# A three-layer fp32 kernel on one core: five chunks of the modulation vectors by 512-column matmuls with silu(c) spread over the array, turned by VectorE, and twelve matmuls of constants at the start

## The chip, the cores and the metric

The kernel runs on one core of one Trainium2 chip. The metric is the device time of the whole program in microseconds. The program issues its instructions to TensorE (PE), VectorE (DVE), ScalarE (ACT), GpSimd (POOL) and SyncE (SP, which issues most transfers). All data are float32. Each fp32 matmul in the program shows in the trace as two matmul instructions, so counts of the trace are twice those of the program.

## What is computed

256 tokens of width 1024 go through three blocks. In each, a conditioning vector `c` gives shift, scale and gate vectors by a matrix, and these modulate the normed input:

```python
def first_block(x, c, w_mod, b_mod, ...):
    mod = silu(c) @ w_mod + b_mod                       # [1,1024] @ [1024,6144]
    shift1, scale1, gate1, shift2, scale2, gate2 = split(mod, 6)
    h = rms_norm(x, g_pre_mix) * (1 + scale1) + shift1
    y = hybrid_mixer(h, w_in, ...)                      # attention and gated linear attention
    x = x + gate1 * rms_norm(y, g_post_mix)
    h = rms_norm(x, g_pre_ffn) * (1 + scale2) + shift2
    y = moe_ffn(h, router_w, ...)                       # 32 experts, 4 per token
    return x + gate2 * rms_norm(y, g_post_ffn)
# the second block (mod = silu(c_2) @ w_ada_2 + b_ada_2, 3072 columns) and the third
# (two layers, silu(c_3) @ ada_w_3[l] + ada_b_3[l], 6144 columns each) have the same frame
# with other mixers and feed-forward parts
```

## The kernel before

The program is written by hand, engine by engine; each engine's instructions run in the order in which they are written, and semaphores join the engines (`e.wait_ge(*at(name))` waits for the instruction that was counted under that name). The stages come one after the other: `start`, `first` (the first block's mixer), `moe` (its experts), `second`, `even`, `ffn0`, `odd`, `ffn1`. The profile's lines for TensorE's dense matmuls are L792 (token-major, 512 columns) and L776 (feature-major, 256 columns); L735, L1152, L883 and L1208 are transposes; L1007, L1015 and L996 are the attention's.

**Modulation chunks.** The columns of all `mod` matrices that are needed are cut into chunks of 512, `ADA[0]`, `ADA[1]`, ... A chunk's weights are 1024 x 512, 2 MB, laid in a slot of the weight ring as 8 tiles of 128 rows (k = 0 to 7). A chunk is computed in one of two ways:

- By VectorE: `ada_acc_dve` multiplies the 8 tiles with silu(c) as a per-partition scalar and adds them (L608, L611, L616). TensorE then sums over the partitions with a vector of ones in `ada_sum_pe` (L625, four matmuls of one column each for a chunk of kind "cols").
- By TensorE alone, `ada_columns_pe` (L648): for each of the 4 groups of 128 columns and each of the 8 k, the 128 x 128 piece of weights is the stationary operand and one column of silu(c) is the moving one. So a chunk is 32 matmuls of one column, 64 in the trace. Chunks 1, 12, 13 and 15 are done so, and half of chunk 3 (columns 0 to 255; VectorE does the other half).

Both leave the chunk with its 128 features on the partitions, in four columns of a PSUM bank. `ada_put_dve` then adds the bias and puts it into `MOD` (L669, L672, L675).

**Chunk places.** Chunks 0 to 3 are the first block's first shift and scale; the `first` stage starts when they are there: `first_put_act` and `first_put_dve` (L475, L482) apply them to the turned input, and the small matmul L776 on `GR` (the gate's low rank projection) is the first that reads that. Chunk 12's two halves stand in the attention of token block 1 (`first_piece_pe`, s = 5 and s = 8), chunk 13's around a transpose after the linear attention (`first_pe`), and chunk 15's first half between the two norms' transposes (L883) at the end of `first`; its last two quarters stand after the router (L1979) and after the ranks (L1984 to L1988) in `moe_pe`, ahead of the first gather (L1521) of the experts.

**Weight ring and banks.** SP loads the weights into four slots in the order of use, each load waiting until the slot's last reader is done; for the experts two more slots are used, the tiles `GR` and `AUX`. The 4th load of expert weights takes the slot of chunk 15, and the loads into `GR` and `AUX` are queued behind it. PSUM's 8 banks are handed out in turn, and a bank waits for the readers of its last user.

**ACT's start.** ACT issues half of the small transfers of vectors, takes silu(c) from the turned `c` in the middle of them (L452), and issues the transfer `GR<-in_w_in` last (L457). POOL issues the other half. TensorE turns the vectors when all have landed (L498), behind chunk 1 and the sum of chunk 0.

Of the kernel before, what the change touches and what calls it, by code (L numbers as in the profile page):

```python
# [373 lines left out]
def programs(T, out, m, ps, sems, slots, at_c, at):  # L374
# [16 lines left out]
    GLRW = GR[:, 2, 0:128].rearrange("p (k n) -> p k n", k=8)  # L391
    VC = GR[0:24, 4, NV * 128:NV * 128 + 128]
# [49 lines left out]
    def start_act(e):  # L442
# [6 lines left out]
        for i, (dst, src, cleared) in enumerate(vector_pieces(0)):  # L449
            if i == N_PIECES[0] // 2:  # L450
                e.wait_ge(*at("c turned"))
                e.activation(CS[:, :], bank("c")[:, 0:24], ACT.Silu).then_inc(*act("cs"))  # L452
                act.leave("bank", "c")
            if cleared:
# [14 lines left out]
        act.name("first", "act")  # L469
        inputs_landed(e)  # L470

# [14 lines left out]
    def start_pe(e):  # L486
# [3 lines left out]
        e.wait_ge(*at("cs"))  # L490
        ada_columns_pe(e, 1, range(4))
        ada_sum_pe(e, 0)
        vectors_landed(e)
        e.wait_ge(*at("vr cleared"))
        for i in range(0, NV, 4):
# [3 lines left out]
            ins.then_inc(*pe("vectors turned", i))  # L499
        e.wait_ge(*at("first", "xn"))  # L500
        turn_pe(e, "first", lambda t, k: m.first.XN[:, t, cols(k)], 8)
        ada_sum_pe(e, 2)
        ada_columns_pe(e, 3, (0, 1))
        e.wait_ge(*at("ada acc", 3))
        for f in range(2, 4):
            ins = e.matmul(bank("ada", 3)[:, f:f + 1], AC2[:, 0, cols(f)], ones[:, 0:1], start=True, stop=True,
                           skip_group_check=True)
        ins.then_inc(*pe("ada summed", 3))
        bank.drop("ada", 3)
# [75 lines left out]
    BY_COLUMNS = (1, 12, 13, 15)  # L585
    SIDE, BEFORE, last_of = {}, {}, {}
    for n in range(len(ADA)):
        if n not in BY_COLUMNS:
# [50 lines left out]
    def ada_columns_pe(e, n, fs):  # L639

        w = ring.tile(1024, 512, "ada", n)
        if fs[0] == 0:
            bank.take(e, "ada", n, hold=True)
            e.wait_ge(*at("w", "ada", n))
        b = bank("ada", n)
        for f in fs:
            for k in range(8):
                ins = e.matmul(b[:, f:f + 1], w[:, k, cols(f)], CS[:, ADA[n][3] + k:ADA[n][3] + k + 1], start=k == 0, stop=k == 7,  # L648
                               skip_group_check=True)
        if n == 3:  # L650
            ins.then_inc(*pe())
            pe.leave("w", "ada", n)
        elif fs[-1] == 3:
            ins.then_inc(*pe("ada summed", n))
            pe.leave("w", "ada", n)
            bank.drop("ada", n)

    def ada_put_dve(e, n):
        kind, _, _, _, j, rest, _ = ADA[n]
        b = bank("ada", n)  # L660
        e.wait_ge(*at("ada summed", n))
        if kind == "cols":
# [5 lines left out]
            if j < 2:  # L668
                e.tensor_tensor(o, b[:, 0:4], bv, ADD).then_inc(*dve())  # L669
                dve.leave("bank", "ada", n)  # L670
            else:
                e.scalar_tensor_tensor(out=o, in0=b[:, 0:4], scalar=1.0, in1=bv, op0=ADD, op1=ADD).then_inc(*dve())  # L672
                dve.leave("bank", "ada", n)
                own(e, dve)
# [413 lines left out]
    wi1 = T["w_in"][0]  # L1088
    R1, U1 = F1.XN[:, :, 0:512], F1.XN[:, :, 512:768]
# [2135 lines left out]
```

## Time and profile before

| | |
|---|---|
| median of 3 runs | 2635.36 us (2631.52 to 2641.18) |
| profiled execution, its own time | 2640.11 us |
| its span in the trace | 2638.3 us |
| TensorE busy | 2353.4 us, 89% of the span |
| VectorE busy | 844.8 us, 32% |
| ScalarE busy | 412.4 us, 16% |
| mean granted TensorE clock | 0.931 of full |
| moved by DMA | 655.50 MB, mean 248 GB/s |

The chain of work that ended last is TensorE's for the greater part. Between about 330 us and 1330 us the 16 DMA engines are busy 91% to all of the time with the experts' weights; ahead of that and behind it TensorE is busy nearly without a gap. The granted clock is one of two levels: 1.00 is 2.4 GHz, 0.50 is 1.2 GHz.

### The profile page before, as it was taken

Reading aid. Unit: us, or ns where it says so; the run is one execution under the profiler, and the core shown is the slowest. Engines: PE = TensorE matmul, PEld = TensorE weight load, DVE = VectorE, ACT = ScalarE, POOL = GpSimd, SP = SyncE. Lnnn points to the kernel's source line nnn. Section 1 sums busy time; section 2 is a strip of 40 time slices with the busy share of each in tenths; the row PEclk is TensorE's granted clock in tenths of the full one; section 3 lists DMA queues with packets and bytes.
Section 4 is the critical chain, followed back from the end, with each engine's and each line's share of the span. In section 5 each row is a group of like instructions: output and inputs, shape, how many; then the busy total and the mean of one; then the engine's idle time right before and its main releaser. Section 6 shows DMA issues by size and latency. Waiting matters only on the chain. (4 is left out here: it accounts for less than half of the span.)

```text
span 2638.3 us, 25405 instructions
## 1 busy us (share of the span) xinstructions
PE 2353.4 (89%) x9952; PEld 1375.0 (52%) x9952; DVE 844.8 (32%) x1734; ACT 412.4 (16%) x889; POOL 115.9 (4%) x81
## 2 busy tenths in 40 slices
PE   6998989888899888888879989898779998989998
PEld 5565633333333333333337678655648763646873
DVE  4554312211122111122236443643366301332301
ACT  1212201111111111111122311112221001221100
POOL 1000000001000010000000000000300000000000
PEclk9977799999999999999989998889889999989999
DMA  8753468999989999999976720464236543323441
GB/s 314 263 217 138 177 245 322 381 412 406 411 305 378 409 397 412 403 409 412 401 300 248 255 80 17 179 247 179 96 128 235 180 152 126 132 86 120 160 143 65
DMA packets 212255, 655.50 MB, mean 248 GB/s; under 512 B 8518, under 2 KB 13182, under 8 KB 195540
## 3 DMA queue, kind: packets, MB, share of 16 engines
q1 hardware_dynamic: 208368, 647.86, 64.8%
q0 software_dynamic: 1712, 3.60, 0.4%
q8 instruction: 119, 1.95, 0.3%
q10 hardware_dynamic: 2004, 1.67, 0.2%
q14 instruction: 52, 0.43, 0.0%
HBM read 652.05 MB, written 1.05 MB: 248 GB/s over the span
## 5 line engine op out<-in xcount | busy, mean ns | idle before, releaser
L1558 PE MATMUL ps<-w,XE 128*64 128x512 f32 x1536 | 363.0, 628 | 66.5 <-DMA w<-in_w_gate_up 63.0
L776 PE MATMUL ps<-HF,w 128*128 128x256 f32 x1408 | 312.7, 385 | 1.8 <-DVE CF L2854 1.8
L776 PEld LDWEIGHTS ps<-HF,w 128*128 128x128 f32 x1408 | 271.8, 194 | 43.6 <-issue 5.7
L1558 PEld LDWEIGHTS ps<-w,XE 128*64 128x64 f32 x1536 | 122.8, 144 | 292.5 <-issue 288.5
L1588 DVE TENSOR_TENSOR T<-ps,BB 128x512 f32<-128x512 f32 x64 | 44.3, 692 | 616.9 <-PE ps L1558 616.9
L611 DVE SCALAR_TENSOR_TENSOR AUX<-w,CS,AUX 128x512 f32<-128x512 f32 (+1 forms) x228 | 169.8, 745 | 8.1
L792 PE MATMUL ps<-w,AF 128*128 128x512 f32 x352 | 151.6, 593 | 1.8 <-DVE AF L2876 1.8
L792 PE MATMUL ps<-w,HT 128*128 128x512 f32 (+1 forms) x352 | 152.8, 589 | 0.3 <-DVE S L1403 0.3
L776 PE MATMUL ps<-HT,w 128*128 128x256 f32 x640 | 146.8, 388 | 5.5 <-DVE dqk L2291 3.7
L1629 PE MATMUL ps<-GR,AT 128*64 128x512 f32 x256 | 120.9, 628 | 31.4 <-DMA AUX<-in_w_down 31.1
L1629 PE MATMUL ps<-w,AT 128*64 128x512 f32 x512 | 121.8, 619 | 18.3 <-DMA w<-in_w_down 17.9
L776 PEld LDWEIGHTS ps<-HT,w 128*128 128x128 f32 x640 | 123.0, 195 | 25.8 <-issue 9.0
L1629 PE MATMUL ps<-AUX,AT 128*64 128x512 f32 x256 | 121.4, 630 | 0.0
L1493 POOL PARTITION_BROADCAST BB<-BR x32 | 73.6, 2299 | 967.3 <-DMA BR<-in_b_gate_up 948.7
L1558 PE MATMUL ps<-GR,XE 128*64 128x512 f32 x256 | 113.3, 595 | 0.4 <-DVE ACCM L1666 0.4
L1558 PE MATMUL ps<-AUX,XE 128*64 128x512 f32 x256 | 113.3, 595 | 0.0
L792 PEld LDWEIGHTS ps<-w,AF 128*128 128x128 f32 x352 | 66.7, 190 | 85.9 <-issue 83.2
L792 PEld LDWEIGHTS ps<-w,HT 128*128 128x128 f32 x352 | 67.0, 202 | 75.8 <-issue 75.1
L1598 ACT ACTIVATE T<-T 128x256 f32<-128x256 f32 x70 | 30.8, 441 | 441.6 <-DVE T L1571 441.6
L1629 PEld LDWEIGHTS ps<-GR,AT 128*64 128x64 f32 x256 | 35.6, 144 | 108.6 <-issue 108.6
L792 PE MATMUL ps<-w,HO 128*128 128x512 f32 x192 | 85.6, 604 | 1.0 <-ACT st L846 1.0
L1629 PEld LDWEIGHTS ps<-w,AT 128*64 128x64 f32 x512 | 39.7, 141 | 88.3 <-issue 78.6
(568 smaller groups left out, 2666.9 us busy)
## 6 DMA issues: line engine op xcount, KB each, us to landing
w<-in_w_gate_up SPq DMA_DIRECT2D x96, 2048.0 KB, 15.7
w<-in_w_down SPq DMA_DIRECT2D x32, 2048.0 KB, 19.3
w<-in_ada_w SPq DMA_DIRECT2D x24, 2048.0 KB, 7.9
w<-in_ffn_w_in SPq DMA_DIRECT2D x20, 2048.0 KB, 7.9
w<-in_w_in SPq DMA_DIRECT2D x17, 2048.0 KB, 9.3
GR<-in_w_gate_up SPq DMA_DIRECT2D x16, 2048.0 KB, 18.1
AUX<-in_w_gate_up SPq DMA_DIRECT2D x16, 2048.0 KB, 22.8
GR<-in_w_down SPq DMA_DIRECT2D x16, 2048.0 KB, 10.0
```

What stands on the lines that cost most here:

```text
L611: e.scalar_tensor_tensor(out=acc, in0=w[:, k, lo:], scalar=c, in1=acc, op0=MUL, op1=ADD).then_inc(*dve())
L776: ins = e.matmul(out_, w[:, k, c:c + n], HT[:, k, :], start=k == 0, stop=k == kc - 1, skip_group_check=True)
L792: ins = e.matmul(out_, HT[:, k0 + k, cols(t)], w[:, k, c:c + n], start=start and k == 0, stop=stop and k == kc - 1, skip_group_check=True)
L1493: e.partition_broadcast(FM.BB[0:n, :], FM.BR[32 * j:32 * j + 1, :], n).then_inc(*pool(x, "bias"))
L1558: ins = e.matmul(b[j * n:j * n + n, :], FM.XE[:, side(x), 4 * kh + k, j * n:j * n + n], ring.tile(512, 1024, "gu", ex_, h, kh, x[0])[:, k, ...
L1588: e.tensor_tensor(FM.T1[:, :], bank(x, "gu", q), FM.BB[:, q * 512:q * 512 + 512], ADD).then_inc(*dve())
L1598: e.activation(FM.T2[:, :], v[:, :, 0], ACT.Sigmoid, scale=1.702).then_inc(*(wide["act"] if len(key) > 1 else act)(x, "sig", *key))
L1629: ins = e.matmul(b[j * n:j * n + n, :], FM.AT[:, 4 * d + k, j * n:j * n + n], ring.tile(512, 1024, "down", ex_, d, x[0])[:, k, 512 * hf:51 ...
```

## The change

Chunks 1, 12, 13, 15 and the half of chunk 3 are computed with the operands exchanged. ScalarE spreads silu(c) into a tile `CSB` (part of `GR`): for each k a block of 128 x 128 in which all 128 columns are the same column of silu(c). That block is stationary and the weights' tile of 128 x 512 (256 for chunk 3) is moving. A chunk is then 8 matmuls of 512 columns, which leave its 512 values in each partition of a whole bank. VectorE takes them out of it by four fused multiplies with the identity, summed along the row (`ada_turn_dve`), into four columns of `st`, ahead of the former `ada_put_dve`.

With it come:

- ScalarE writes `CSB` for silu(c) between the small transfers, and for silu(c_2) after chunk 3 (`spread_act`); it copies it into `CSB2` (the tile `att_p`, which is not used any more by then) in `first_act` after the first head norm, for chunk 15.
- 12 matmuls of constants with 256 columns stand on TensorE behind the transpose of `c`. Nothing reads their result.
- On TensorE the turned vectors go ahead of chunk 1.
- The sum of chunk 3's second half gets a bank of its own ("3b"), copied to `st` by VectorE.
- Chunk 12's two parts are k = 0 to 3 and k = 4 to 7, chunk 13's too; chunk 15's three parts are k = 0 to 2, 3 to 5 and 6 to 7, at the same places.

```diff
@@ start_act
                 e.activation(CS[:, :], bank("c")[:, 0:24], ACT.Silu).then_inc(*act("cs"))
                 act.leave("bank", "c")
+                own(e, act)
+                spread_act(e, 0, CSB)
...
         act.name("first", "act")
+        e.wait_ge(*at("ada summed", 3))
+        spread_act(e, 8, CSB)
         inputs_landed(e)
+    def spread_act(e, ccol, dst):
+        e.activation(dst, CS[:, ccol:ccol + 8].unsqueeze(2).broadcast_to([128, 8, 128]), ACT.Copy).then_inc(
+            *act("spread", ccol))
@@ start_pe
         e.transpose(b[:, 0:24], VC, ident[0:24, 0:24]).then_inc(*pe("c turned"))
-        e.wait_ge(*at("cs"))
-        ada_columns_pe(e, 1, range(4))
-        ada_sum_pe(e, 0)
+        b = bank.take(e, "warm")
+        for _ in range(12):
+            ins = e.matmul(b[:, 0:256], ident, CT[:, 0:256], start=True, stop=True, skip_group_check=True)
+        ins.then_inc(*pe())
+        pe.leave("bank", "warm")
         vectors_landed(e)
...
             ins.then_inc(*pe("vectors turned", i))
+        e.wait_ge(*at("spread", 0))
+        ada_rows_pe(e, 1, CSB)
+        ada_sum_pe(e, 0)
         e.wait_ge(*at("first", "xn"))
         turn_pe(e, "first", lambda t, k: m.first.XN[:, t, cols(k)], 8)
         ada_sum_pe(e, 2)
-        ada_columns_pe(e, 3, (0, 1))
+        ada_rows_pe(e, 3, CSB, n_cols=256)
+        b = bank.take(e, "ada", "3b")
         e.wait_ge(*at("ada acc", 3))
@@
-    def ada_columns_pe(e, n, fs):
+    def ada_rows_pe(e, n, spread, ks=range(8), n_cols=512):
         w = ring.tile(1024, 512, "ada", n)
-        if fs[0] == 0:
+        if ks[0] == 0:
             bank.take(e, "ada", n, hold=True)
             e.wait_ge(*at("w", "ada", n))
...
+        for k in ks:
+            ins = e.matmul(bank("ada", n)[:, 0:n_cols], spread[:, k, :], w[:, k, 0:n_cols], start=k == 0, stop=k == 7,
+                           skip_group_check=True)
+        if ks[-1] == 7:
+            ins.then_inc(*pe("ada rows", n))
+            if n_cols == 512:
+                pe.name("ada summed", n)
             pe.leave("w", "ada", n)
             bank.drop("ada", n)
+
+    def ada_turn_dve(e, n, fs):
+        e.wait_ge(*at("ada rows", n))
+        for f in fs:
+            e.tensor_tensor_reduce(TURN if n < 15 else m.moe.T2[:, 0:128], bank("ada", n)[:, cols(f)], ident, 1.0, 0.0, MUL, ADD, st[:, 50 + f:51 + f]).then_inc(
+                *dve())
+            own(e, dve)
+        dve.leave("bank", "ada", n)
 
     def ada_put_dve(e, n):
         b = bank("ada", n)
+        if n in BY_ROWS:
+            ada_turn_dve(e, n, range(2 if n == 3 else 4))
+            b = st[:, 50:54]
         e.wait_ge(*at("ada summed", n))
+        if n == 3:
+            e.tensor_copy(st[:, 52:54], bank("ada", "3b")[:, 2:4]).then_inc(*dve())
+            dve.leave("bank", "ada", "3b")
+            own(e, dve)
@@ first_piece_pe
-            ada_columns_pe(e, 12, (0, 1))
+            e.wait_ge(*at("spread", 8))
+            ada_rows_pe(e, 12, CSB, range(4))
...
-            ada_columns_pe(e, 12, (2, 3))
+            ada_rows_pe(e, 12, CSB, range(4, 8))
@@ first_pe
-        ada_columns_pe(e, 13, (0, 1))
+        ada_rows_pe(e, 13, CSB, range(4))
         e.wait_ge(*at("hn1", 0, "out"))
         turn_half_pe(e, "gla turned", 0, 512)
-        ada_columns_pe(e, 13, (2, 3))
+        ada_rows_pe(e, 13, CSB, range(4, 8))
...
         norm_turn_pe(e, m.moe, "moe", 0)
-        ada_columns_pe(e, 15, (0, 1))
+        e.wait_ge(*at("spread", "again"))
+        ada_rows_pe(e, 15, CSB2, range(3))
         norm_turn_pe(e, m.moe, "moe", 1)
@@ first_act
             headnorm_act(e, ("hn1", t), F1.XN[:, t, 0:512], 4, F1.XN[:, 0, 512:1024], st[:, 44 + 4 * t:48 + 4 * t])
+            if t == 0:
+                e.activation(CSB2, CSB, ACT.Copy).then_inc(*act("spread", "again"))
@@ moe_pe
-        ada_columns_pe(e, 15, (2,))
+        ada_rows_pe(e, 15, CSB2, (3, 4, 5))
         b = bank.take(e, "ranks")
...
-        ada_columns_pe(e, 15, (3,))
+        ada_rows_pe(e, 15, CSB2, (6, 7))
```

On TensorE the program before begins with these rows (the program's own counts, half of the trace's; `w_2` is chunk 1's slot, `w_4` chunk 3's):

```order
L489 MATMUL ps<-CT,GR 128x24
L648 MATMUL ps<-CS,w_2 128x1 x32
L625 MATMUL ps<-CT,AUX 128x1 x4
L498 MATMUL ps<-CT,GR 128x128 x5
L735 MATMUL ps<-CT,XN 128x128 x16
L625 MATMUL ps<-CT,AUX 128x1 x4
L648 MATMUL ps<-CS,w_4 128x1 x16
L506 MATMUL ps<-CT,AUX 128x1 x2
L776 MATMUL ps<-HT,GR 16x256 x8
```

The changed program begins on TensorE so:

```order
L499 MATMUL ps<-CT,GR 128x24
L502 MATMUL ps<-CT 128x256 x12
L510 MATMUL ps<-CT,GR 128x128 x5
L660 MATMUL ps<-w_2,GR 128x512 x8
L639 MATMUL ps<-CT,AUX 128x1 x4
L763 MATMUL ps<-CT,XN 128x128 x16
L639 MATMUL ps<-CT,AUX 128x1 x4
L660 MATMUL ps<-w_4,GR 128x256 x8
L522 MATMUL ps<-CT,AUX 128x1 x2
L804 MATMUL ps<-HT,GR 16x256 x8
```

The vectors' transposes moved ahead of chunk 1, and the matmuls of one column became matmuls of 512 and 256. From the router on, TensorE's rows before are these (L1979 is the router, L1984 to L1988 the ranks, L1521 the gather):

```order
L1979 MATMUL ps<-RW,HT_41 128x32 x16
L648 MATMUL ps<-CS,w_1 128x1 x8
L1984 MATMUL ps<-sl,CT 128x32
L1985 MATMUL ps<-sl,CT 128x32
L1986 MATMUL ps<-sl,CT 128x32
L1987 MATMUL ps<-sl,CT 128x32
L1988 MATMUL ps<-sl,CT 128x32
L648 MATMUL ps<-CS,w_1 128x1 x8
L1521 MATMUL ps<-PG,XN_40 128x128 x16
```

In the changed program the same place reads:

```order
L2012 MATMUL ps<-RW,HT_41 128x32 x16
L660 MATMUL ps<-w_1,att_p 128x512 x3
L2017 MATMUL ps<-sl,CT 128x32
L2018 MATMUL ps<-sl,CT 128x32
L2019 MATMUL ps<-sl,CT 128x32
L2020 MATMUL ps<-sl,CT 128x32
L2021 MATMUL ps<-sl,CT 128x32
L660 MATMUL ps<-w_1,att_p 128x512 x2
L1554 MATMUL ps<-PG,XN_40 128x128 x16
```

Nothing moved there; the parts of chunk 15 stand where they stood, in three and two matmuls. On VectorE the start of the changed program has these rows where the one before had two `TENSOR_TENSOR MOD<-ps,VT` in a row (L673 is the multiply with the identity and the read of its sum; L696 puts chunks 0 and 1, L698 and L703 chunk 2):

```order
L696 TENSOR_TENSOR MOD<-ps,VT 128x4
L673 ISA GR,st<-ps,CT 128x128
L673 ISA st 128x1
L673 ISA GR,st<-ps,CT 128x128
L673 ISA st 128x1
L673 ISA GR,st<-ps,CT 128x128
L673 ISA st 128x1
L673 ISA GR,st<-ps,CT 128x128
L673 ISA st 128x1
L696 TENSOR_TENSOR MOD<-st,VT 128x4
L698 SCALAR_TENSOR_TENSOR MOD<-ps,VT 128x4
L703 TENSOR_TENSOR MOD<-MOD,VT 128x4
```

The four multiplies are queued between the put of chunk 0 and that of chunk 2.

## Rows read from the trace of the kernel before

**Rows 1.** The page: TensorE's granted clock in 40 equal slices.

```profile
PEclk9977799999999999999989998889889999989999
```

**Rows 2.** Timeline of TensorE, 8 to 70 us: start us, us, engine line operation.

```profile
20.40 13.79 PE L648 MATMUL ps<-CS,w 128*128 128x1 f32 x64 [11.70 <-DMA w<-in_w_mod]
...
39.96 0.95 PE L625 MATMUL ps<-CT,AUX 128*128 128x1 f32 x8
...
49.52 5.45 PE L776 MATMUL ps<-HT,GR 128*16 128x256 f32 x16 [2.01 <-ACT HT L475]
54.90 14.00 PE L792 MATMUL ps<-w,HT 128*128 128x512 f32 x32
```

**Rows 3.** Timeline of VectorE, 20 to 50 us.

```profile
31.56 0.69 DVE L616 TENSOR_TENSOR AUX<-AUX 128x512 f32<-128x512 f32 x1
...
40.94 0.16 DVE L672 SCALAR_TENSOR_TENSOR MOD<-ps,VT 128x4 f32<-128x4 f32 x1 [2.96 <-PE ps L625]
```

**Rows 4.** Windows: stretch, us, busy (instructions) of PE, PEld, DVE, ACT, POOL, clock, DMA, GB/s.

```profile
43.00:53.00 10.00, 7.18 (x27) 4.80 (x27) 4.55 (x11) 1.02 (x2) 0.00 (x0) 0.50 1.05 387
55.00:69.00 14.00, 14.00 (x33) 6.07 (x34) 8.83 (x17) 0.00 (x0) 0.00 (x0) 1.00 0.13 50
...
183.00:189.00 6.00, 6.00 (x39) 4.53 (x37) 4.46 (x7) 0.00 (x0) 0.00 (x0) 1.00 0.24 49
190.00:203.00 13.00, 11.94 (x43) 8.45 (x45) 3.17 (x6) 1.19 (x2) 0.00 (x0) 0.50 0.71 268
...
224.00:233.00 9.00, 9.00 (x34) 7.45 (x34) 4.61 (x8) 1.32 (x3) 0.00 (x0) 0.50 0.19 41
...
252.00:284.00 32.00, 25.73 (x120) 25.36 (x121) 11.77 (x47) 5.74 (x16) 6.22 (x5) 0.50 0.26 75
298.00:314.00 16.00, 15.70 (x74) 5.41 (x73) 5.33 (x12) 4.92 (x12) 0.00 (x0) 1.00 0.01 5
```

**Rows 5.** DMA by queue (queue, kind: packets, MB, share), 22 to 24 us.

```profile
q10 hardware_dynamic: 1, 0.00, 0.0%
```

**Rows 6.** Timeline of TensorE, 155 to 204 us.

```profile
170.09 4.54 PE L648 MATMUL ps<-CS,w 128*128 128x1 f32 x32 [0.58 <-DVE att_m L1045]
...
175.38 5.68 PE L792 MATMUL ps<-w,HT 128*128 128x512 f32 x8
...
186.89 4.17 PE L648 MATMUL ps<-CS,w 128*128 128x1 f32 x32
190.92 1.95 PE L1015 MATMUL ps<-va,att_p 128*128 128x64 f32 x8
```

**Rows 7.** Timeline of TensorE, 216 to 290 us.

```profile
219.66 3.63 PE L648 MATMUL ps<-CS,w 128*128 128x1 f32 x32
...
223.62 6.54 PE L648 MATMUL ps<-CS,w 128*128 128x1 f32 x32
230.02 5.74 PE L792 MATMUL ps<-w,HT 128*128 128x512 f32 x8
...
255.25 1.95 PE L883 MATMUL ps<-CT,XN 128*128 128x128 f32 x8
263.47 7.01 PE L1979 MATMUL ps<-RW,HT 128*128 128x32 f32 x32 [6.27 <-issue]
270.29 3.55 PE L648 MATMUL ps<-CS,w 128*128 128x1 f32 x16
...
279.25 6.73 PE L1521 MATMUL ps<-PG,XN 128*128 128x128 f32 x32
```

**Rows 8.** Timeline of VectorE, 216 to 281 us.

```profile
227.05 0.69 DVE L1083 TENSOR_TENSOR O<-O,rg 128x512 f32<-128x512 f32 x1
...
253.66 1.29 DVE L876 TENSOR_SCALAR XN<-X,st 128x512 f32<-128x512 f32 x2
...
272.65 0.19 DVE L2054 CUSTOM_DVE_ANT_0 G<-w,sl 128x32 f32<-128x32 f32 x1
...
276.06 0.19 DVE L2063 SCALAR_TENSOR_TENSOR rk<-ps,sl 128x32 f32<-128x32 f32 x1 [1.93 <-PE ps L1988]
```

## The prediction on record

> **What bounds the kernel now.** I first read the page's clock line [rows 1]: nearly everywhere TensorE is granted nine tenths or all of full speed, but slices 3 to 5 (132 to 330 us) show 7. The changed chunks stand there and at the start, so I read TensorE's timeline from 0 to 290 us [rows 2, 6, 7]. From 20 us to 255 us TensorE is the engine that sets the end: its own gaps are a few of 1 to 2 us, the largest being the wait for the first weights up to 20.40 and 2.01 us for ScalarE at 49.52 [rows 2]. Then I cut the same time into windows for the clock [rows 4]. It is at 1.00 in the dense stretch 55 to 69 us and at 183 to 189, and at 0.50 (1.2 GHz) at 43 to 53, 190 to 203, 224 to 233 and 252 to 284 us. Each of these begins about 2 to 4 us after one-column matmuls L648 began: at 40.8 us behind the row of L625 at 39.96, at 186.89, at 219.66 and between the two transposes of L883 [rows 2, 6, 7]. TensorE was busy for all 6 us of 183 to 189, and the level fell all the same. Behind that, at half rate, stand dense matmuls that cost more than they would: the 8 of L792 at 230.02 took 5.74 us, where 32 at full rate took 14.00 us, 3.5 us for 8 [rows 2, 7].
>
> What the experts add is a question of where the stream of their weights starts. At 298 to 314 us the DMA engines stand still, share 0.01, while TensorE works 15.70 of 16 us [rows 4]: the slots are full, and their release by TensorE sets when the stream goes on. So what TensorE gains before 298 us moves the whole stream and reaches the end.
>
> **The price of a chunk itself** hardly changes. A half chunk by columns is 32 instructions: 3.63 us at full rate (113 ns each) [rows 7]; at half rate 13.79 / 64 = 215 ns each, 6.9 us [rows 2]. A half chunk by rows is 8 instructions of 512 columns, at full rate 14.00 / 32 = 437 ns each [rows 2], 3.5 us; at 1.2 GHz twice that, 7.0 us. The profile's clock reads 1.00 from 20 to 34 us, before its first record, but a one-column matmul that takes 215 ns there and 113 ns later says that this is 1.2 GHz. So what counts is at which level a chunk runs and what level it leaves behind. Dense work of this form (L792, full rows, 512 columns) holds 1.00 for as long as it runs [rows 4]; I take it that rows of chunks do the same.
>
> **Start.** Before: chunk 1 from 20.40 to 34.1, the sum of chunk 0, the vectors and the input turned, the sum of chunk 2 at 39.96 to 40.9; VectorE puts chunk 2 at 40.94 [rows 2, 3]; 49.52 is 8.6 us later. After: the constants' 24 instructions of 256 columns cost 24 x 0.22 = 5.3 us at full and 10.5 us at half rate, from about 8.7 us, so they end between 14 and 19.2 us, ahead of 20.4, when chunk 1's weights are there (that wait is a DMA's and stays). The vectors: ScalarE's queue q10 has one packet left after 22 us [rows 5], and its last issue, 1024 small pieces of `w_in`, is behind the vectors; so they land before 22 us, most likely by 17, the 1.1 us by which the spread delays them included. Bound: if at 23, 3.5 us are lost. I take 17, and the five transposes are done before 20.4. Chunk 1 by rows is then 16 x 0.437 = 7.0 us at full rate; the gap of some 2 us after the constants may let the level fall, and then about 4 us pass at half rate, 9 us in all. So it ends at 27.4 to 29.4. The sum of chunk 0 (0.95 us) and 16 transposes at full rate (about 2.1) end at 30.5 to 32.5, and the sum of chunk 2 can't start before VectorE has it at 31.56 + 0.69 = 32.25 [rows 3]. It ends at 33.3, instead of 40.9: 7.6 us, 7.2 with the unlucky phase. From there the chain is as before but for VectorE's additions in it: two multiplies with the identity of chunk 3 in place of TensorE's wait and one copy. The nearest row is the fused multiply of 128x32 at 0.19 us, next instruction after 0.23 [rows 8], the upper bound a 128x512 operation at 0.69 us [rows 3]; I take 0.35 us each for 128x128 and lose 0.5 us in all (0.2 to 1.2). The four of chunk 1, 1.4 us, lie in the 2 us in which VectorE waits for the sum of chunk 2. **Start: -6.9 us** (-3.4 to -7.5).
>
> **Chunk 12.** First half at 170.09: 4.54 us become 3.5, and L792 behind it 5.68 becomes 3.5, since the level doesn't fall; with the small attention pieces between, 10.8 us become 7.6: -3.2. Second half at 186.89: 4.17 becomes 3.5, -0.6. Behind it, from 190.92 to about 199.5, stand the attention's last pieces and a row sum at half rate [rows 4, 6] that would take 4.7 us at full. But they are thin themselves, so the level may fall again within them: -2.7 of the possible -4. TensorE's short wait for VectorE's `O` behind them stays. VectorE's four multiplies (1.4 us, at most 2.8) stand before its copy of `att_p`, and TensorE has 3.7 us of other work before it needs that. **-6.5 us** (-3.2, if only the first half's effect comes, to -9).
>
> **Chunk 13.** First half 3.63 against 3.5. Second half 6.54 becomes 3.5, and L792 behind it 5.74 becomes 3.5 [rows 7]. VectorE's head norm, which these wait for, is done at 227.05 + 0.69 = 227.7 [rows 8]; the transpose that needs it comes at 223.6 + 7.0 = 230.6. ScalarE's copy into `CSB2` (1 us) lies in a wait. **-5.0 us** (0 to -5.3).
>
> **Chunk 15.** Its first part lies in the wait for VectorE's L876 (253.66 to 254.95) and saves only that TensorE comes 0.3 us late at 255.25 and transposes in 1.95 us for about 1.05: **-1.0 us** (0 to -1.2). The second part is on the path, since VectorE waits 1.93 us for the ranks behind it [rows 8]. The router before it is thin and leaves the level at half, as now [rows 4, 7]. Six instructions of rows at half rate for about 4 us and then full: 4.6 us, instead of 3.4: +1.2. If the level then is full, the ranks take 1.2 for 2.1 us, the last part 1.75 for 3.4, and the gather (6.73 us) about 4.2. From the ranks' end VectorE needs 1.9 us for what the gather waits for, so it begins 0.2 us after the last part; all in all TensorE ends the gather 3.5 us earlier. If the level rises only within the gather, it is -0.5, and if never, +2. **-2.5 us** (+2 to -3.5).
>
> **Sum.** 6.9 + 6.5 + 5.0 + 1.0 + 2.5 = 21.9 us. Against the profiled execution: 2640.1 - 21.9 = 2618.2 us. That execution is 4.75 us above the median of the runs, so in terms of the median 2635.4 - 21.9 = 2613.5, and I say 2614.
>
> **A rule against it.** TensorE was busy in 6.00 of the 6 us ahead of 189 us, and the level was 0.50 directly after [rows 4]. The Trainium skill, "TensorE: Matmul & The Clock Gate", Part 1, says that the gate follows how busy TensorE has been, and that sustained activity releases the throttle. By that rule taken plainly a one-column stream is as good as a dense one, and the change buys nothing but its rearrangement. The trace here disagrees, if "busy" means the engine's busy time, but it leaves open why the level falls.
>
> **Rivals.**
>
> (a) *The levels stay where they are*: something other than the chunks lets the level fall (the thin attention pieces, the norms). Then at the start chunk 1 costs 14.0 us at half rate and only the five transposes of the vectors move out of the path (1.2 us by the 8 in 1.95 us [rows 7]), less 0.5 on VectorE; chunk 12 is 0; chunk 13 +0.5 (7.0 for 6.54); chunk 15 +1.9 and +0.1. Total +1.8 us: 2637. The thin L1015 and L1007 behind 186.89 speak for it, the 1.00 under L792 from 55 to 69 us, and the fall behind each of the four streams of L648 alike, against it. The rule above would give this one. Chance 7%.
>
> (b) *Part of it*: the start and chunk 13 come (11.9 us), but in chunk 12's and 15's surroundings thin work drops the level anyway: 2635.4 - 12 = 2623, or 2619 to 2627. For it: L1007, L1015, L996, the router are all thin. Chance 22%.
>
> (c) *Slower*: full-array matmuls that start from half rate don't raise it soon. If all halves of 12, 13 and 15 run at 7.0 us and so does each L792 of 8 behind them, chunk 12 costs 14.0 for 8.7 plus 1.3 + 3.4 us behind it, chunk 13 14.0 for 10.2 plus 1.3, chunk 15 +2; with a start of -1 that is +15 us: 2650. It decides from the point at which less than a third of the rows run at full rate. Against it: L792 holds 1.00 over 14 us [rows 4], and the level rose under L776 and L792 after 49.52. Chance 4%.
>
> (d) *Hidden*: the experts' stream starts by something that isn't moved, so that what comes after 280 us keeps its time. Then nothing remains, 2635. The idle DMA at 298 to 314 us speaks against it. Chance 4%.
>
> **Numbers.** The forecast holds 63%, (a) to (d) the 37% left. A difference under 0.5%, 13.2 us, is about what a measurement of this kernel can't tell from none. Its own range is 2606 (26 us, all best ends) to 2621; (b) reaches to 2627, and a range to there leaves (a), (c) and (d) out, 15%; at its low end it goes to 2605. Faster by over 0.5% (under 2622) is all of the forecast and six tenths of (b): 0.76; same is the rest of (b), (a), (d), and a quarter of (c): 0.21; slower 0.03.
>
> **What would show it.** Features of `first` (L804 now) start at 42 to 43 us; the first chunk's matmuls L660 at 20.4 us last 7 to 9 us; clock 1.00 from there through 190 less 7 us, and no stretch of 0.50 between the two halves of chunk 13 and the expert norm; the gather ends by about 264 instead of 286 us; the DMA's idle stretch before the experts' stream shifts by the same 22 us, and from then on the two traces run in parallel. I am wrong if the constants or the vectors end after 20.4 us, if VectorE's multiplies take over 0.7 us each, or if the level falls during the rows.

## The result: 1.0% faster, ratio 0.9899

The changed kernel takes 2607.05 us, the median of 4 runs (2603.8 to 2615.2), against 2633.44 us for the one before in the same comparison. The ratio is 0.9899, with a 95% interval of 0.9868 to 0.9931. The forecast was 2614 us (2605 to 2627), 21.4 us under the median of before; measured are 26.4. A second set of 6 runs of the changed kernel on another occasion gave 2612.32 us against 2635.32, 23.0 us less, a ratio of 0.9907 (0.9881 to 0.9933).

The profiled execution took 2603.8 us with a span of 2602.0, 36.3 us less than the span before. Only 22.6 us of that come from the stretch that the change touches; where the rest comes from is told behind the experiments.

### The profile page after: what moved, and what is told of

Same layout as the page of the kernel before. It is cut to its first block and busy times, and to the rows that moved or that the text cites. A ratio compares the mean times of both kernels' runs of the same rounds, so it can differ in the third digit from the quotient of the medians.

```text
span 2602.0 us, 25084 instructions
## 1 busy us (share of the span) xinstructions
PE 2324.2 (89%) x9768; PEld 1330.8 (51%) x9768; DVE 850.8 (33%) x1771; ACT 415.1 (16%) x892; POOL 115.8 (4%) x81
## 5 line engine op out<-in xcount | busy, mean ns | idle before, releaser
L1591 PE MATMUL ps<-w,XE 128*64 128x512 f32 x1536 | 362.5, 627 | 66.4 <-DMA w<-in_w_gate_up 63.0
L1591 PEld LDWEIGHTS ps<-w,XE 128*64 128x64 f32 x1536 | 124.3, 144 | 290.3 <-issue 286.4
L820 PE MATMUL ps<-w,AF 128*128 128x512 f32 x352 | 151.6, 593 | 1.8 <-DVE AF L2909 1.8
L820 PE MATMUL ps<-w,HT 128*128 128x512 f32 (+1 forms) x352 | 147.1, 572 | 0.3 <-DVE S L1436 0.3
L804 PEld LDWEIGHTS ps<-HT,w 128*128 128x128 f32 x640 | 124.1, 197 | 26.3 <-issue 9.1
L1591 PE MATMUL ps<-GR,XE 128*64 128x512 f32 x256 | 113.3, 595 | 0.4 <-DVE ACCM L1699 0.4
L1591 PE MATMUL ps<-AUX,XE 128*64 128x512 f32 x256 | 113.3, 595 | 0.0
L820 PEld LDWEIGHTS ps<-w,AF 128*128 128x128 f32 x352 | 66.7, 190 | 85.9 <-issue 83.2
L820 PEld LDWEIGHTS ps<-w,HT 128*128 128x128 f32 x352 | 64.7, 195 | 72.8 <-issue 72.0
L1662 PEld LDWEIGHTS ps<-GR,AT 128*64 128x64 f32 x256 | 36.3, 147 | 106.8 <-issue 106.8
L820 PE MATMUL ps<-w,HO 128*128 128x512 f32 x192 | 85.6, 604 | 1.0 <-ACT st L874 1.0
## 6 DMA issues: line engine op xcount, KB each, us to landing
AUX<-in_w_gate_up SPq DMA_DIRECT2D x16, 2048.0 KB, 22.2
```

Of the source, the lines that this page charges most:

```text
L804: ins = e.matmul(out_, w[:, k, c:c + n], HT[:, k, :], start=k == 0, stop=k == kc - 1, skip_group_check=True)
L820: ins = e.matmul(out_, HT[:, k0 + k, cols(t)], w[:, k, c:c + n], start=start and k == 0, stop=stop and k == kc - 1, skip_group_check=True)
L1591: ins = e.matmul(b[j * n:j * n + n, :], FM.XE[:, side(x), 4 * kh + k, j * n:j * n + n], ring.tile(512, 1024, "gu", ex_, h, kh, x[0])[:, k, ...
L1662: ins = e.matmul(b[j * n:j * n + n, :], FM.AT[:, 4 * d + k, j * n:j * n + n], ring.tile(512, 1024, "down", ex_, d, x[0])[:, k, 512 * hf:51 ...
```

## The profile after

The mean granted clock is 0.943 in place of 0.931. The page's clock line, in 40 equal slices, against [rows 1]:

```profile
PEclk9998999999999999999989989999789999989999
```

Slices 3 to 5 went from 7 to 9 or 8; a 7 further back, in slice 29, is new.

TensorE's timeline from 0 to 50 us, as in [rows 2] (start us, us, engine line operation, idle before and what ended it):

```profile
8.65 7.85 PE L502 MATMUL ps<-CT 128*128 128x256 f32 x24
17.07 0.77 PE L510 MATMUL ps<-CT,GR 128*128 128x128 f32 x5 [0.57 <-DMA GR<-in_ffn_conv_b]
20.57 8.70 PE L660 MATMUL ps<-w,GR 128*128 128x512 f32 x16 [2.73 <-DMA w<-in_w_mod]
...
32.55 1.02 PE L639 MATMUL ps<-CT,AUX 128*128 128x1 f32 x8 [0.69 <-DVE MOD L696]
...
42.20 6.31 PE L804 MATMUL ps<-HT,GR 128*16 128x256 f32 x16 [2.18 <-ACT HT L485]
```

The features start at 42.20 instead of 49.52, 7.3 us earlier. The vectors' last transfer ends TensorE's wait at 17.07, and they are turned before chunk 1's weights are there at 20.57. VectorE's part, by its timeline from 32 to 41 us:

```profile
32.40 0.28 DVE L673 CUSTOM_DVE_ANT_0 GR<-ps,CT 128x128 f32<-128x128 f32 x1
...
32.72 0.29 DVE L673 CUSTOM_DVE_ANT_0 GR<-ps,CT 128x128 f32<-128x128 f32 x1
```

One multiply with the identity starts 0.32 us behind the other; four take 1.3 us.

The windows of the changed kernel (columns as in [rows 4]):

```profile
20.00:22.00 2.00, 1.43 (x2) 0.84 (x3) 0.99 (x2) 0.00 (x0) 0.00 (x0) 0.59 1.10 362
24.00:40.00 16.00, 13.01 (x65) 9.12 (x63) 13.02 (x36) 1.02 (x2) 0.00 (x0) 1.00 1.04 387
42.00:46.00 4.00, 3.80 (x10) 1.34 (x11) 0.00 (x0) 0.68 (x1) 0.00 (x0) 0.50 1.07 390
...
160.00:162.00 2.00, 0.00 (x0) 0.00 (x0) 0.00 (x0) 2.00 (x9) 0.00 (x0) 0.58 1.04 385
168.00:186.00 18.00, 17.89 (x72) 9.82 (x71) 10.15 (x23) 0.00 (x0) 0.00 (x0) 1.00 0.38 131
188.00:190.00 2.00, 1.96 (x10) 1.66 (x10) 1.29 (x2) 0.60 (x1) 0.00 (x0) 0.50 1.03 418
192.00:236.00 44.00, 40.96 (x164) 20.45 (x160) 26.86 (x68) 14.48 (x37) 0.00 (x0) 1.00 0.46 168
240.00:255.00 15.00, 10.55 (x37) 8.51 (x38) 4.65 (x28) 1.93 (x3) 1.58 (x3) 0.50 0.10 20
256.00:264.00 8.00, 7.24 (x49) 5.51 (x47) 6.13 (x20) 2.09 (x6) 4.54 (x2) 1.00 0.44 111
```

From 160 to 162 us TensorE stands still, and the level falls. From 168 to 186 us, with the second half of chunk 12 in it, the level is 1.00, and only behind that it falls for some 3 us. The stretch of 44 us at 1.00 from 192 to 236 us holds all of chunk 13; before, the same work had 0.50 for 9 us [rows 4]. The router and the second part of chunk 15 run at 0.50 as before. Now the timeline from 150 to 265 us, against [rows 6, 7]:

```profile
163.67 5.40 PE L660 MATMUL ps<-w,GR 128*128 128x512 f32 x8 [7.10 <-DMA w<-in_w_ada]
...
178.78 3.60 PE L660 MATMUL ps<-w,GR 128*128 128x512 f32 x8
...
207.31 3.60 PE L660 MATMUL ps<-w,GR 128*128 128x512 f32 x8
...
211.18 3.60 PE L660 MATMUL ps<-w,GR 128*128 128x512 f32 x8
214.62 3.60 PE L820 MATMUL ps<-w,HT 128*128 128x512 f32 x8
...
236.93 1.24 PE L911 MATMUL ps<-CT,XN 128*128 128x128 f32 x8 [1.89 <-DVE XN L904]
244.45 7.01 PE L2012 MATMUL ps<-RW,HT 128*128 128x32 f32 x32 [6.28 <-issue]
251.27 5.11 PE L660 MATMUL ps<-w,att_p 128*128 128x512 f32 x6
...
259.57 3.81 PE L1554 MATMUL ps<-PG,XN 128*128 128x128 f32 x32 [0.35 <-DVE mxc L2103]
```

The first line is new: TensorE is ready for chunk 12 at 156.6 us and waits 7.10 us for its weights. SyncE's timeline shows when they are issued:

```profile
148.66 0.37 SPq L194 DMA_DIRECT2D w<-in_w_out  x1
149.07 29.43 SPq L194 DMA_DIRECT2D w<-in_w_ada  x3
```

They stand directly behind 2 MB of `w_out`, and both have to come in; the row in [rows 6] had 0.58 us of wait at the same place. The half chunk behind the wait begins at half rate and takes 5.40 us.

## The experiments

Two numbers are read from each run besides the time: when the first gather starts (279.25 us before [rows 7]), and when SyncE issues the last load of an expert's weights into `GR` (1329.48 us before, 1303.61 in the changed kernel). The second is behind all that the change touches and before the stages that follow.

**The change without its constants.**

```diff
-        b = bank.take(e, "warm")
-        for _ in range(12):
-            ins = e.matmul(b[:, 0:256], ident, CT[:, 0:256], ...)
```

> The change without its 12 matmuls of constants. Theory 1 (the constants buy nothing): in the changed kernel the clock is back at half rate within 2 us after they and the vectors' transposes end, and stands at 0.59 and 0.55 in the first 4 us of chunk 1, as it would without them. Then chunk 1 starts at about 20.6 us and takes 8.7 to 9.6 us, and the features' first matmul (L776 before, L804 after) starts within 1 us of 42.2 us; time equal to the change, 2604 to 2610. Theory 2 (they keep the clock up for chunk 1): chunk 1 takes 12 us or more, the features start at 45 us or later, and the time is 3 us or more above the change.

Measured: 2613.48 us, ratio 0.9915 (0.9894 to 0.9936). Its timeline of TensorE:

```profile
17.17 1.33 PE L505 MATMUL ps<-CT,GR 128*128 128x128 f32 x5 [8.50 <-DMA GR<-in_ffn_conv_b]
20.49 9.62 PE L655 MATMUL ps<-w,GR 128*128 128x512 f32 x16 [1.99 <-DMA w<-in_w_mod]
...
42.55 5.32 PE L799 MATMUL ps<-HT,GR 128*16 128x256 f32 x16 [2.18 <-ACT HT L485]
```

Chunk 1 takes 9.62 us in place of 8.70, and the features start at 42.55 in place of 42.20. Even this isn't the constants' doing: with them chunk 1 took between 8.70 and 10.17 us in the profiles of the eight kernels here that have the same start. The last load is issued at 1302.89 us, no later than in the changed kernel, and the ratio lies within the intervals of the change. Theory 1 holds: the constants buy nothing that can be seen. The time itself, 2613.48 us, is above the 2604 to 2610 that was expected, but the kernel before was slower on that occasion too (2638.65 against 2633.44 us), so the ratio is what compares.

**The start alone**, chunks 12, 13 and 15 by columns:

```diff
-            ada_rows_pe(e, 12, CSB, range(4))
+            ada_columns_pe(e, 12, (0, 1))
```

and so for the other halves.

> Only the start of the change: chunks 1 and 3 by rows, constants and vectors ahead; chunks 12, 13 and 15 by columns as before. Theory 1 (the gains of the two places add): the features start at 42.2 us as in the change and the time is about 7 us under before, 2626 to 2629. Theory 2 (the earlier start is taken back later by a wait for weights, as the changed kernel waits 7.1 us for chunk 12's): TensorE comes to chunk 12 at most 6 us earlier than before and the time is within 3 us of before.

**The later part alone**, the start as before:

```diff
-        ada_rows_pe(e, 1, CSB)
+        ada_columns_pe(e, 1, range(4))
```

with the order of before, and chunk 3 by columns.

> Only the later part of the change: the start as before, chunks 12, 13 and 15 by rows. Theory 1 (the level of the clock): the first gather ends about 15 us earlier than before, the gap between this and the whole change is the start's 7 us, and the time is 2612 to 2616. Theory 2 (the later gain needs the earlier start's phase of the clock): less than 8 us under before, 2625 or more.

Measured: the start alone 2625.07 us, 0.9945 (0.9925 to 0.9965); the later part alone 2620.5 us, 0.9923 (0.9903 to 0.9943). The two ratios together make 0.9868, the whole change measured 0.9899 and 0.9907, so they add within their intervals. The traces say more about where. From the start alone, TensorE:

```profile
42.55 5.36 PE L821 MATMUL ps<-HT,GR 128*16 128x256 f32 x16 [2.18 <-ACT HT L483]
...
164.30 5.79 PE L676 MATMUL ps<-CS,w 128*128 128x1 f32 x32 [1.86 <-DMA w<-in_w_ada]
...
274.20 5.74 PE L1567 MATMUL ps<-PG,XN 128*128 128x128 f32 x32
```

Of 7.0 us at the features 5.8 are left at chunk 12 and 5.1 at the gather. From the later part alone:

```profile
51.71 5.33 PE L812 MATMUL ps<-HT,GR 128*16 128x256 f32 x16 [1.92 <-ACT HT L483]
...
172.20 3.67 PE L653 MATMUL ps<-w,GR 128*128 128x512 f32 x8 [0.63 <-DMA w<-in_w_ada]
...
266.34 2.05 PE L1562 MATMUL ps<-PG,XN 128*128 128x128 f32 x16
```

Here the features start 2.2 us later than before though the program is the same up to there (the level of the clock fell at another place), and the gather starts 12.9 us earlier: 15.1 us come between the two. By these rows both theories 1 hold: each part gives its own gain, and the later one doesn't need the earlier.

The times fit less well. The start alone was expected 7 us under before; 0.9945 is 14.5 us (9 to 20), while its profile has 5.1 us at the gather. That profile is of the slowest of the six runs, 11 us above their median. The later part alone was expected at 2612 to 2616 and took 2620.5, in ratio 20 us (15 to 26), with the gather's end 14.0 us earlier in the trace. What fills these gaps isn't shown; how much the stretches behind the change vary by themselves is told further below.

**Wide columns.** The operands are turned back, the weights' pieces stationary, 32 matmuls a chunk as before; what moves is a block of 128 equal columns of silu(c). VectorE copies four columns.

```diff
-        for k in ks:
-            ins = e.matmul(bank("ada", n)[:, 0:n_cols], spread[:, k, :], w[:, k, 0:n_cols], ...)
+        for f in fs:
+            for k in range(8):
+                ins = e.matmul(bank("ada", n)[:, cols(f)], w[:, k, cols(f)], spread[:, k, :], ...)
```

> The change with the operands turned back: the weights' 128x128 pieces are stationary again, 32 matmuls a chunk as before, but each moves the 128 equal columns of the spread silu(c) in place of one column. VectorE copies four columns out of the bank in place of four multiplies. Theory 1 (what counts is that the stream is dense, so that the clock stays at full rate behind it): a half chunk of 12 or 13 takes 3.5 to 3.8 us, the clock is 1.00 between the two halves of chunk 13 and behind them, and the time is that of the change within 4 us, 2603 to 2611. Theory 2 (what counts is fewer matmuls and weight loads): the time goes back towards that of the start alone, 2620 or more.

Measured: 2613.38 us, ratio 0.9899 (0.988 to 0.9919). A window of the clock, and TensorE's timeline:

```profile
192.00:236.00 44.00, 41.20 (x225) 26.61 (x223) 25.53 (x57) 14.51 (x37) 0.00 (x0) 1.00 0.47 170
```

```profile
20.48 9.01 PE L661 MATMUL ps<-GR,w 128*128 128x128 f32 x64 [2.78 <-DMA w<-in_w_mod]
...
206.05 3.73 PE L661 MATMUL ps<-GR,w 128*128 128x128 f32 x32
...
210.06 3.74 PE L661 MATMUL ps<-GR,w 128*128 128x128 f32 x32
...
259.41 3.81 PE L1556 MATMUL ps<-PG,XN 128*128 128x128 f32 x32
```

This is the experiment that decides. A half chunk has the same 32 instructions and weight loads as before and costs the same, 3.73 us against 3.63 at full rate [rows 7]; yet the level stays at 1.00 between the halves and behind them, and the gather starts at 259.41 us, where the changed kernel's starts at 259.57. So the gain is not in fewer matmuls or weight loads. It is in the level of the clock. At chunk 13 this holds in every profile: in the eleven with rows or wide columns both halves take 3.60 to 3.74 us and the eight dense matmuls behind them 3.60; in the two with one column (before and the start alone) the second half takes 6.54 and 5.88 us and the eight behind it 5.74 and 6.42. Chunk 1 is a second pair: the same 64 instructions took 13.79 us with one column, 215 ns each on average [rows 2], and 9.01 us with 128, so the wide stream also brings the level up within itself. (The constants stand ahead of the latter, but by rows chunk 1 took 9.62 us without them.) Between one and 128 columns no width was tried.

The Trainium skill ("TensorE: Matmul & The Clock Gate", Part 1) says that the gate follows how busy TensorE is. If that means the engine's busy time, this pair disagrees: TensorE was busy in 6.00 of 6 us ahead of a fall and in 9.00 of 9 us at 0.50 [rows 4], and here in 41.20 of 44 us at 1.00. The time of 2613.38 us is 2.4 above the 2603 to 2611 that was expected; the ratio is the change's.

**The change once more**, beside the next three.

> The changed kernel itself, to stand beside the three that follow on the same chip. Both theories expect 2604 to 2615 us, a ratio to before of 0.988 to 0.992. If TensorE comes to chunk 12 before about 158 us it waits for the weights there until 163 to 164 us; if it comes at 161 to 163 us, because the clock was at half rate shortly before, it waits 1 us or less, and the two cases meet again.

Measured: 2612.32 us, ratio 0.9907 (0.9881 to 0.9933). Its row at chunk 12:

```profile
163.26 3.67 PE L660 MATMUL ps<-w,GR 128*128 128x512 f32 x8 [0.67 <-DMA w<-in_w_ada]
```

Here the level had fallen at the attention's thin pieces, TensorE came 6 us later, waited 0.67 us in place of 7.10 and was at chunk 12 0.4 us earlier, with the clock at full rate. The wait for the weights swallows what TensorE gains ahead of it.

**Chunk 12's weights first.**

```diff
+        ada_load(e, 12)
         ring.load(e, T["w_out"][0][0:512, :], 512, 1024, "out1", 0)
-        for n in (12, 13, 14):
+        for n in (13, 14):
             ada_load(e, n)
-        ring.skip()
         ring.load(e, T["w_out"][0][512:1024, :], 512, 1024, "out1", 1)
+        ring.skip()
```

> The change with chunk 12's weights loaded ahead of the first half of w_out in place of behind it (the two trade slots). Theory 1 (TensorE's 7.1 us wait at chunk 12 is the DMA's two loads in a row, 2 MB each at about 390 GB/s): the weights land 5 us earlier, TensorE's wait for them is under 2 us, and the first gather starts 1 us (when TensorE comes late by the clock) to 5 us (when it comes early) earlier than in the change. Theory 2 (the wait only moves to w_out, needed 4 us later): gain under 1 us.

Measured: 2603.3 us, ratio 0.9872 (0.9847 to 0.9896). Its timeline of TensorE:

```profile
156.59 3.67 PE L660 MATMUL ps<-w,GR 128*128 128x512 f32 x8 [0.33 <-DMA w<-in_w_ada]
161.67 0.63 PE L1035 MATMUL ps<-CT,att_s 128*128 128x128 f32 x4 [1.40 <-ACT att_s L1059]
...
252.16 3.81 PE L1555 MATMUL ps<-PG,XN 128*128 128x128 f32 x32 [0.35 <-DVE mxc L2104]
```

The wait for the weights is 0.33 us, ScalarE's exponentials are next with 1.40 us, and the gather starts 7.4 us earlier than in the first profile of the change and 5.5 us earlier than in the second. Theory 1 holds in its cause; in size it is more than the 1 to 5 us expected, because the weights are there some 7 us earlier instead of 5 (156.6 against 163.3 to 163.7 us) and the level doesn't fall in a wait, so the half chunk takes 3.67 us in place of 5.40.

**Constants ahead of the router**, in TensorE's wait of 6.3 us (12 matmuls of 256 columns):

```diff
         norm_turn_pe(e, m.moe, "moe", 1)
+        fill_pe(e, 12, "router")
         end(pe, "pe", "first")
```

> The change plus 12 matmuls of constants of 256 columns behind the last transposes of the expert norm, in the 6.3 us in which TensorE waits for the router's weights. Nothing reads them. Theory 1 (the level of the clock is what the end of this stage costs): router 3.6 in place of 7.0 us and the second part of chunk 15 2.6 in place of 5.1 us, the first gather starts 5 to 6 us earlier, and so does the end: 2599 to 2609. Theory 2 (thin router matmuls drop the level anyway before they are done, or VectorE's choice of experts is behind): less than 2 us.

Measured: 2611.99 us, ratio 0.9915 (0.9892 to 0.9937): no gain. Timeline of TensorE:

```profile
238.19 5.35 PE L673 MATMUL ps<-CT 128*128 128x256 f32 x24
248.16 7.00 PE L2021 MATMUL ps<-RW,HT 128*128 128x32 f32 x32 [4.63 <-issue]
```

The router starts 3.7 us later than in the change, and at half rate, since the level falls in the 4.63 us of wait that are left. POOL issues the router's weights when TensorE's last instruction of the stage is counted, and the constants stood ahead of that mark: it issues 6.7 us behind the start of the last transposes in place of 3.2, so 3.5 us are lost (the next expectation says 5). This miss is of my placing, not of either theory. So once more behind the mark:

```diff
         end(pe, "pe", "first")
+        fill_pe(e, 12, "router")
```

> The 12 matmuls of constants again, in the wait ahead of the router, but behind the mark that POOL waits for before it issues the router's weights; in the run before they stood ahead of that mark and held the transfer back by 5 us. Theory 1 (level of the clock): POOL issues at the same 3.1 us behind the last transposes as in the change, the router takes 3.6 to 5 us in place of 7.0, the second part of chunk 15 2.7 in place of 5.1 to 5.5, and the first gather starts 4 to 6 us earlier against the last transposes than in the change (there 22.6 us behind their start). Theory 2 (the router's thin matmuls drop the level again within their first microseconds, or VectorE is behind): 1 us or less.

Measured: 2605.18 us, ratio 0.9878 (0.9858 to 0.9899).

```profile
235.40 5.35 PE L673 MATMUL ps<-CT 128*128 128x256 f32 x24
241.80 5.32 PE L2021 MATMUL ps<-RW,HT 128*128 128x32 f32 x32 [1.05 <-issue]
246.93 4.58 PE L660 MATMUL ps<-w,att_p 128*128 128x512 f32 x6
...
254.40 3.84 PE L1563 MATMUL ps<-PG,XN 128*128 128x128 f32 x32
```

From the last transposes' start to the gather it is 254.40 - 234.33 = 20.1 us, in the change 22.6 and 23.0: 2.5 to 2.9 us gained, less than the 4 to 6 of theory 1. The router begins at full rate and ends at half (5.32 us, between 3.6 and 7.0), and chunk 15's part has 4.58 us. Both theories are right in part: the thin router lets the level fall within it.

**Constants ahead of the features**, 5 and 4 matmuls in the two waits of 2.3 and 2.2 us:

```diff
         ada_rows_pe(e, 3, CSB, n_cols=256)
+        fill_pe(e, 5, "a")
...
         ins.then_inc(*pe("ada summed", 3))
+        fill_pe(e, 4, "b")
```

> The change plus 5 and 4 matmuls of constants of 256 columns in TensorE's two waits ahead of the first features (2.3 us for VectorE's half of chunk 3 and 2.2 us for ScalarE). Theory 1: the level is held at 1.00 and the first features and the dense matmuls behind them start at full rate, 3.7 in place of 6.3 us; every load after it is issued 2.5 us earlier; the time falls by 2 to 3 us. Theory 2 (it comes back in the wait for chunk 12's weights): TensorE is 2.5 us earlier up to there and nothing is left at the first gather.

Measured: 2609.27 us, ratio 0.9898 (0.9871 to 0.9926).

```profile
42.35 3.61 PE L814 MATMUL ps<-HT,GR 128*16 128x256 f32 x16 [0.35 <-issue]
...
161.21 6.29 PE L662 MATMUL ps<-w,GR 128*128 128x512 f32 x8 [5.58 <-DMA w<-in_w_ada]
...
257.97 3.84 PE L1564 MATMUL ps<-PG,XN 128*128 128x128 f32 x32
```

The features take 3.61 us in place of 6.31 (or 5.33 in the second profile of the change), chunk 12 comes 2.1 to 2.5 us earlier, and the gather at 257.97 lies between the change's two, 257.69 and 259.57. In time nothing can be told from the change.

**All three together**, by rows and by wide columns: the weights of chunk 12 first, and both sets of constants.

> The change with chunk 12's weights first, the constants ahead of the features, and the constants behind the mark ahead of the router. Theory 1: the three add, about 5 + 2.5 + 4 us against the change at the first gather, and the time is 2595 to 2603. Theory 2: chunk 12's weights are the limit again, since TensorE comes earlier but the load is issued by slots that DMA and VectorE set: no better than chunk 12's weights first alone, 2603.

> The same three, with the chunks as weights stationary and 128 equal columns of silu(c) moving. Theory 1 (dense is what counts): within 3 us of the kernel with rows; VectorE's put is 1 us shorter. Theory 2: rows are better by more than 5 us.

Measured: by rows 2608.88 us, 0.9886 (0.9868 to 0.9903); by wide columns 2600.95 us, 0.9874 (0.9853 to 0.9895). They don't add: the gathers start at 253.31 and 252.61 us, where one piece, the weights first, reached 252.16. Theory 1 of the combination is out. So is the cause that theory 2 names, for TensorE waits only 0.19 us for chunk 12's weights at 155.10. In the kernel by rows chunk 12 starts at 155.10, 1.5 us ahead of the weights-first kernel, but the level falls behind its second half. One window of it:

```profile
184.00:189.00 5.00, 5.00 (x26) 2.57 (x19) 4.53 (x16) 0.00 (x0) 0.00 (x0) 0.50 0.00 0
```

And the same window of the kernel with the weights first:

```profile
184.00:189.00 5.00, 4.53 (x23) 2.17 (x20) 4.53 (x16) 0.00 (x0) 0.00 (x0) 1.00 0.02 6
```

Whether the level falls in those thin stretches differs from run to run of like programs, and costs as much as one of these repairs brings: from chunk 12 to chunk 13 the two combined kernels need 45.5 and 46.0 us, the one with the weights first 42.1.

A second loss is at the router. In all three kernels with the weights first it starts 8.9 to 9.4 us behind the start of the last transposes, in the change 7.5. POOL issues its weights 3.2 us behind them in all of these, but with the weights first they land after 3.9 to 4.0 us in place of 2.3, and the DMA engines are busy all of the first 3 us of that (share 1.0; in the change under 0.1 in the first microsecond behind the issue). So the constants ahead of the router gain 0.7 to 1.2 us (22.7 and 23.1 us to the gather, against 23.8 without them) and not 2.5.

By wide columns the median is 7.9 us lower than by rows, where 3 were expected at most; the gathers differ by 0.7 us and the intervals overlap, so nothing is to be read from it.

The ratios of the three fastest kernels, 0.9872, 0.9874 and 0.9878, are 0.2 to 0.35 points under the change's 0.9899 and 0.9907, but their intervals overlap with the change's. That the weights first save 5 us or more, and the constants behind the mark 2.5, is read from the traces and not from these ratios.

## Where the rest of the 36 us comes from

SyncE's issue of the same loads, before and after, gives how far ahead the changed kernel is: 22.6 us where the stream of experts goes on (314.11 against 291.50), 22.2 us at 350, 25.9 us at 1329.48, 26.3 us at 1543.45. Then, in the second block's stage, which no edit touches, it becomes 35.8 us by 1683.56. Windows of 40 us over the same work, first before:

```profile
1620.00:1660.00 40.00, 33.08 (x167) 25.13 (x166) 8.77 (x21) 5.97 (x10) 0.00 (x0) 0.67 0.00 0
```

and after, 26.3 us earlier:

```profile
1593.70:1633.70 40.00, 30.68 (x193) 23.18 (x191) 9.46 (x23) 7.83 (x13) 0.00 (x0) 0.91 0.00 1
```

The level happened to be at 0.67 in one and 0.91 in the other; 9.5 us of the profiled pair are chance. Between the same two loads (1543.45 and 1683.56 before) the kernel before needs 140.1 us, the changed kernel 130.6 in its first profile and 140.9 in its second, which has a level of 0.68 over the same 40 us. Over all thirteen profiles it is 130.6 to 141.5 us, and no edit touches anything there. The experts' stretch varies too. From 350 us to the last load into `GR` it took 979.1 us before, 975.4 and 976.6 in the changed kernel, and 971.9 to 983.3 over the thirteen, so the 3.7 us won in it can't be told from chance either.

The difference of the medians, 26.4 us, agrees with the 26 us that the traces show ahead of that place; in the second set it is 23.0, and the second profile is 21.5 us ahead there. The lead at the start of the experts, 22.6 us and in the second profile 24.5, is what the change is shown to give.

## Why the prediction was right, point by point

- **Start**, forecast -6.9: measured -7.3 at the features. The constants ended at 16.5 us and the vectors landed at 17.1, both ahead of 20.4 as assumed; chunk 1 took 8.70 within 7 to 9. VectorE's four multiplies, taken at 1.4 us, took 1.3. TensorE waited 0.69 us for VectorE at the sum of chunk 2, whose end was forecast at 33.3 and came at 33.6. The features themselves ran at half rate for longer, 6.31 for 5.45 us, so 6.5 us were left behind them.
- **Chunk 12**, forecast -6.5: from 6.5 us ahead at 54.90 [rows 2] to 12.35 us at L1238 (188.04; before 200.39), -5.9. Here the forecast left out a wait, and luck hid it. TensorE was ready for chunk 12 at 156.57 us, before at 169.51: 12.9 us ahead, because the level stayed up where it had fallen at 149 and again at 159 us. These 6.5 us were not forecast. The wait of 7.10 us in place of 0.58 took exactly that back, and the first half began at 163.67, 6.4 us ahead, as if only the start had been won. From there the step "10.8 us become 7.6" came to 9.1, -1.7 in place of -3.2, since the wait had let the level fall and the half chunk took 5.40 us and not 3.5. The second half gave -0.6 as forecast, and the thin pieces behind it -3.6 in place of -2.7, since the level stayed at 1.00 until 187 us. So the size is right and its composition is not. The wait could have been seen: [rows 6] names VectorE for the 0.58 us, but TensorE's weight load at that place, at 170.05 us, waited 0.90 us for the DMA of `w_ada`, issued at 157.18, and 12.9 us from issue to first matmul is what the second profile of the change (13.0) and the later part alone (12.95) need when they wait 0.6 us for the same load.
- **Chunk 13**, forecast -5.0: 17.55 us ahead at the expert norm's first transposes (231.39, before 248.94) against 12.35, so -5.2. Both halves 3.60 us and L820 behind them 3.60, as worked out.
- **Chunk 15**, forecasts -1.0 and -2.5: the last transposes took 1.24 for 1.95 us and the router starts 19.0 us ahead, -1.5; the gather and what is behind it end 22.6 us ahead, -3.6. The second part of the chunk took 5.11, not 4.6 us, but the ranks and the gather ran at full rate (3.81 us), and L1591 starts at 264.97 against 287.58 before.
- **Sum**, 21.9: 22.6 at the start of the experts. The stream of weights then kept it; the 3.7 us more by 1330 us were not forecast and lie within what that stretch varies by itself. That the median came 26.4 and not 21.9 us lower is by these traces mostly chance, and 23.0 in the second set is nearer to the sum.
- **Rival (a)**, levels stay where they are, is out by the windows and by the wide columns. **Rival (b)**, thin work drops the level anyway, is true of the router and at times of the attention's last pieces, and it sets how much comes on a given run. **(c)** is out: rows that began at half rate brought the level up, chunk 1 in 8.70 us where 14.0 would be all at half rate, and both halves of chunk 13 took 3.60. **(d)** is out: the experts' loads moved by the full 22.6 us.
- **Signs**: the features at 42.20, chunk 1's 8.70 us, chunk 13's stretch at 1.00 and the gather's end at 263.4 came as named. A clock of 1.00 from chunk 1 up to 183 us did not: it was 0.50 at 42 to 46 us and fell in the wait ahead of chunk 12, and one half chunk of rows began at half rate.
- **Slips in the sums**: the terms of (c) add up to 16.1 and not 15 us, and all best ends are 26.5 us, so 2609 and not 2606. Neither moves the forecast, but the second one helped: the measured 2607.05 us is inside the stated range and 2 us under what the terms themselves allow. In gain, 26.4 against 26.5 us, it is at their edge, and part of it is chance, as shown above.

## What to carry to other kernels

A stream of one-column matmuls is priced not by its own time (3.6 us for a half chunk at full rate here either way) but by the granted clock of what stands behind it: look at the windows behind each such stream, and if they show 0.50, make the moving operand wide, which cost 4 ns a matmul here. What stands behind a wait of several microseconds starts at half rate as well. When TensorE comes earlier to a place, look up when the transfer it needs was issued and what stands ahead of it in the queue; a wait of half a microsecond there before is a warning. Filling instructions belong behind the mark that others wait for.

## What the runs showed that I had not expected

- The same program up to the same place can differ by 2 us at 50 us (49.52 and 51.71 for the features of the two kernels with the old start), and the same changed kernel by 10 us in the second block (130.6 and 140.9 us), by where the level of the clock changes; so a gain under some 5 us is to be read in the trace's rows and not in medians of six.
- With 128 equal columns moving, a matmul with its weight load costs 3.73 / 32 = 117 ns at full rate, against 113 ns with one column: 127 columns more for 4 ns.
